# Two context blocks joined, gate rows by way of DRAM, a conditioning half split over two norms, and another order of MLP pieces

## The reference

```python
x = x + concat(diff_attention, dilated_attention) @ w_out      # first block
x = x + expert_choice_ffn(rms_norm(x))                         # 16 experts, 32 tokens each
x = rms_norm(x)

# second block, two layers i = 0, 1
mod   = silu(c)     @ ada_w[i] + ada_b[i]        # 6 rows of 1024: shift, scale, gate, twice
mod_c = silu(c_ctx) @ ada_w[i] + ada_b[i]
h, hc = x * (1 + sc1) + sh1, ctx * (1 + csc1) + csh1
y, yc = mixer_i(h, hc)                           # i=0: latent attention, i=1: neighbourhood attention
x     = layer_norm(alpha * x + g1 * y)
x     = layer_norm(alpha * x + g2 * mlp(x * (1 + sc2) + sh2))
# the context gets the same two steps in layer 0 only
mlp(h) = square(relu(h @ w1)) @ w2               # 1024 -> 4096 -> 1024
```

## Time and profile before

| | us |
|---|---|
| median of 3 runs (2580.91 to 2585.63) | 2583.34 |
| the profiled execution, its own time | 2582.17 |
| span of that execution in the trace | 2580.1 |

### The profile page before, as it was taken

One profiled execution on the slowest core, in us unless ns is written; L12 is line 12 of the kernel. 1 busy time (PEld: TensorE's weight loads), 2 busy tenths in 40 slices (PEclk: granted clock), 3 DMA queues, 4 the chain that ended last, 5 costly groups with the idle time before them and its releaser, 6 DMA issues.

```text
span 2580.1 us, 27920 instructions
## 1 busy us (share of the span) xinstructions
PE 2227.2 (86%) x11996; PEld 1171.1 (45%) x11996; DVE 534.1 (21%) x1018; ACT 236.8 (9%) x536; POOL 37.8 (1%) x109
## 2 busy tenths in 40 slices
PE   8987888888777888988888876599899999999998
PEld 6544343333333433433433322255466665445665
DVE  1332202221311011011011131224310030163002
ACT  1221101000100000000000000012110000061000
POOL 0000000000000000000000000000020000000000
PEclk9997899999999998999999988999999999999999
DMA  8766979999999999999999999964194431214540
GB/s 311 319 265 240 421 330 410 424 424 422 424 420 419 416 419 415 416 417 416 419 410 418 421 423 425 416 255 177 73 303 149 150 120 65 84 64 148 160 148 33
DMA packets 146564, 786.18 MB, mean 305 GB/s; under 512 B 11187, under 2 KB 66202, under 8 KB 93522
## 3 DMA queue, kind: packets, MB, share of 16 engines
q1 hardware_dynamic: 140104, 774.50, 74.7%
q10 hardware_dynamic: 6346, 9.95, 1.2%
HBM read 783.34 MB, written 6.12 MB: 306 GB/s over the span
## 4 chain that ended last, share of the span: by engine, by line
PE 71%; DMA 15%; DVE 7%; issue 2%; ACT 2%; SPq 2%; ACTq 0%; DVEq 0%
PE ps L285 14%; PE ps L1789 9%; PE ps L2197 9%; PE ps L2204 9%; DMA ring<-in_mlp_w 7%; DMA ring<-in_w_up 6%; PE ps L1757 5%; PE ps L318 4%; PE ps L1947 4%; PE ps L1762 3%; PE ps L1797 2%; PE ps L415 2%; DVE expert_work L1831 2%; PE ps L1809 2%; PE ps L1939 2%
## 5 line engine op out<-in xcount | busy, mean ns | idle before, releaser
L1757 PE MATMUL ps<-ring,xe 128*32 128x512 f32 x2048 | 297.9, 641 | 114.8 <-DMA ring<-in_w_up 41.1
L1789 PE MATMUL ps<-ring,expert_work 128*32 128x512 f32 x1408 | 247.4, 708 | 11.0 <-ACT expert_work L1818 11.0
L1762 PE MATMUL ps<-ring,xe 128*32 128x256 f32 x2048 | 204.9, 462 | 0.0
L1757 PEld LDWEIGHTS ps<-ring,xe 128*32 128x32 f32 x2048 | 61.1, 113 | 226.6 <-issue 97.6
L1762 PEld LDWEIGHTS ps<-ring,xe 128*32 128x32 f32 x2048 | 73.5, 111 | 168.3 <-issue 168.3
L1789 PEld LDWEIGHTS ps<-ring,expert_work 128*32 128x32 f32 x1408 | 60.6, 123 | 162.8 <-issue 140.0
L1947 PE MATMUL ps<-ring,c_qT 128*128 128x512 f32 x256 | 114.1, 598 | 10.3 <-DMA ring<-in_mlp_w 10.1
L1939 PE MATMUL ps<-hT,ring 128*128 128x256 f32 x512 | 114.8, 382 | 6.6 <-DMA ring<-in_mlp_w 6.6
L2197 PE MATMUL ps<-mlp_x_hT,ring 128*128 128x256 f32 x512 | 112.6, 379 | 1.9 <-DVE mlp_x_hT L366 1.9
L2197 PE MATMUL ps<-mlp_n_hT,ring 128*128 128x256 f32 x512 | 112.6, 379 | 1.8 <-DVE mlp_n_hT L366 1.8
L2204 PE MATMUL ps<-ring,mlp_x_h 128*128 128x512 f32 x256 | 111.8, 592 | 0.0
(11 more groups left out here) (399 smaller groups left out, 2118.2 us busy)
## 6 DMA issues: line engine op xcount, KB each, us to landing
ring<-in_w_gate SPq DMA_DIRECT2D x128, 1408.0 KB, 17.2
ring<-in_w_up SPq DMA_DIRECT2D x128, 1408.0 KB, 17.8
ring<-in_w_down SPq DMA_DIRECT2D x112, 1536.0 KB, 23.5
ring<-in_mlp_w SPq DMA_DIRECT2D x96, 1024.0 KB, 9.0
ring<-in_ada_w SPq DMA_DIRECT2D x32, 1536.0 KB, 12.1
ring<-in_w_in SPq DMA_DIRECT2D x8, 1536.0 KB, 19.0
ring<-in_na_w_qkv SPq DMA_DIRECT2D x12, 1024.0 KB, 8.3
ring<-in_w_down SPq DMA_DIRECT2D x16, 512.0 KB, 23.8
```

The source lines that it names most:

```text
L1757: nc.tensor.matmul(ps[32 * j:32 * j + 32, up, :], xe[:, k, :], w[:, :, 4 * j:4 * j + 4], start=(k == 0), stop=(k == KC - 1))
L1762: last = nc.tensor.matmul(ps[32 * j:32 * j + 32, 2, 256 * up:256 * up + 256], xe[:, k, :], two, start=(k == 0 and not up), stop=(k == KC - ...
L1789: last = nc.tensor.matmul(ps[32 * j:32 * j + 32, 1 - half, :], hgT[:, at:at + 32], w[:, (c - c0) * D + 512 * half:(c - c0) * D + 512 * hal ...
```

## The change

Four edits. (a) `uq` is planned behind (1, 3) and run whole after it; `ukv` behind and after (1, 10). (b) The four gates of x are written from `modc` to a DRAM tensor of 4 x 1024 numbers, two by ACT in stage 1, two by SP after NA's projections, and read back into `gB` with one broadcasting DMA each; `gate_jobs` for x is gone (the context's two stay). (c) Of the second conditioning half, pieces 8 to 11 stay behind the output projection; pieces 12 to 15 are planned behind all of mlp_x's pieces and run behind its last matmul, into banks 2 and 3; DVE adds them to the rows after the layer norm, PE waits for that before it transposes x, and the context's transposes use two banks in place of four. (d) `ORDER` takes the four w1 pieces of a turn and then the four w2 pieces, with a wait of PE for the relu and of ACT for the square two groups back.

```diff
+        SPLIT = 12
-        def ada_piece(pe, layer, i, base, bank0):
+        def ada_piece(pe, layer, i, base, bank0, first=0, last_k=KC - 1):
...
-                                        slot(n, N_IN)[:, ADA_W * b:ADA_W * b + ADA_W], start=(k == 0), stop=(k == KC - 1))
+                                        slot(n, N_IN)[:, ADA_W * b:ADA_W * b + ADA_W], start=(k == first), stop=(k == last_k))
...
-        CTX_AFTER = {(0, 8): ("dq",), (0, 12): ("dkv",), (1, 4): ("uq",), (1, 12): ("ukv",),
+        CTX_AFTER = {(0, 8): ("dq",), (0, 12): ("dkv",), (1, 3): ("uq",), (1, 10): ("ukv",),
...
         plan_mla(ids_x, "o")
-        plan_ada(1, 8, 16)
+        plan_ada(1, 8, SPLIT)
         TURN = 4
-        ORDER = [(1, 0), (1, 1), (2, 0), (1, 2), (2, 1), (1, 3), (2, 2), (2, 3)]
+        ORDER = [(1, 0), (1, 1), (1, 2), (1, 3), (2, 0), (2, 1), (2, 2), (2, 3)]
...
         mlp_x = plan_mlp(0)
+        plan_ada(1, SPLIT, 16)
...
+        gate_rows = nc.dram_tensor("gate_rows", [4, D], F32).ap()
+        GATES = ((0, 2), (0, 5), (1, 2), (1, 5))
+        def store_gate(eng, n):
+            layer, which = GATES[n]
+            dst = gate_rows[n:n + 1, :].rearrange("o (c p) -> p (o c)", p=P)
+            src = modc[:, layer, which * KC:which * KC + KC, 0:1].rearrange("p c o -> p (c o)")
+            eng.dma_start(dst, src, allow_slow_non_contiguous=True).then_inc(gate_stored, 16)
+        def load_gate(eng, n, gate):
+            eng.wait_ge(gate_stored, 32 if n < 2 else 64)
+            eng.dma_start(gate[:, :], gate_rows[n:n + 1, :].partition_broadcast(P).rearrange("q o d -> q (o d)"))\
+               .then_inc(gate_loaded.sem, 16)
...
             run_m.ev(act, "act")
+            act.wait_ge(v2.sem, v2.at("mod"))
+            store_gate(act, 0)
+            store_gate(act, 1)
             run_o.finished(act)
...
-                elif at == (1, 4):
-                    lat.pe_q(pe, 0, 4)
-                elif at == (1, 7):
-                    lat.run_uq.pe(pe, 4)
-                elif at == (1, 12):
-                    lat.pe_kv(pe, 0, MLA_HEADS)
-                elif at == (1, 15):
-                    lat.run_ukv.pe(pe, MLA_HEADS)
+                elif at == (1, 3):
+                    lat.pe_q(pe)
+                elif at == (1, 10):
+                    lat.pe_kv(pe)
...  (mixer_end)
-                run_gate.pe(pe)
-                run_gate.finished(pe)
...
-                run_gate.finished(dve)
+                dve.wait_ge(gate_loaded.sem, gate_at)
...  (mlp)
-                run_gate.pe(pe)
-                run_gate.finished(pe)
...
                     n = loop.arrived(pe, m, i)
+                    if g >= 2:
+                        pe.wait_ge(relu_done.sem, m * TURN + (rb + g - 1))
...
+                if beside:
+                    beside.pe_rest(pe)
...
-                run_gate.ev(act, "act")
+                load_gate(act, 2 * layer + 1, gB)
...
+                        if g >= 2:
+                            act.wait_ge(square_done.sem, m * TURN + (qb + g - 1))
...
+                    if beside and t == NT - 1:
+                        beside.dve_rest(dve)
...  (SecondHalf)
             def pe_sum(self, pe):
-                for i in range(KC, 2 * KC):
-                    ada_piece(pe, 1, i, ada1_base, 0)
+                for i in range(KC, SPLIT):
+                    ada_piece(pe, 1, i, ada1_base, 0, 0, SPLIT - KC - 1)
+            def pe_rest(self, pe):
+                for i in range(SPLIT, 2 * KC):
+                    ada_piece(pe, 1, i, ada1_base, 2, SPLIT - KC)
+            def dve_rest(self, dve):
+                dve.wait_ge(ada_done.sem, ada1_base + 2 * KC)
+                dve.wait_ge(self.rows_out, 1)
+                for b in range(2):
+                    row = self.rows[:, b, :]
+                    last = nc.vector.tensor_tensor(row, ps[:, 2 + b, 0:ADA_W], row, ALU.add)
+                last.then_inc(self.rows_out, 1)
...  (NA)
-        run_tc = Run(modulated(1, 0, 1, hT2, 0))
+        run_tc = Run(modulated(1, 0, 1, hT2, 0), (0, 1))
...
             run_tc.finished(pe)
+            pe.wait_ge(second_half.rows_out, 2)
             run_tx.pe(pe, normed)
...
+            run_n.finished(sp)
+            store_gate(sp, 2)
+            store_gate(sp, 3)
+            load_gate(sp, 2, gB)
             feed(sp)
```

More of the change, by code:

```diff
@@ L1293, in build @@
         mlp_n = plan_mlp(1)
+        gate_rows = nc.dram_tensor("gate_rows", [4, D], F32).ap()
+        gate_stored = sem("gate_rows_stored")
+        gate_loaded = Count(sem("gates_loaded"))
+        GATES = ((0, 2), (0, 5), (1, 2), (1, 5))
[8 more added lines that the diff above has]
+               .then_inc(gate_loaded.sem, 16)
+            gate_loaded.take(16)
         keep = ExitStack()
@@ L1310, in build @@
         a2 = Steps(sem("p2_act"), ["row2", "subsd"] + rms_names(NT) + ["ra"])
-        v2 = Steps(sem("p2_dve"), ["row3", "subvar", "sub", "var", "h", "lmax", "aff", "slot", "sel"])
+        v2 = Steps(sem("p2_dve"), ["row3", "subvar", "sub", "mod", "var", "h", "lmax", "aff", "slot", "sel"])
         run_ada = Run(ada_jobs(0, 0, rows0[:, 0:2, :]) + ada_jobs(0, 1, rows0[:, 2:4, :]))
@@ L2103, in mixer_end @@
             run_pre = Run(pre)
-            run_gate = Run(gate_jobs(layer, 2, s, gB), (4, 5))
             run_t = Run(transposes(KC, lambda t, c: o[:, t, c * P:(c + 1) * P], lambda c: oT[:, c, :]) if o is not None else [])
@@ L2107, in mixer_end @@
             a, v = Steps(sem(f"{name}_act"), ["pre", "ln_sd0", "ln_sd1"]), Steps(sem(f"{name}_dve"), ln_names())
+            gate_at = gate_loaded.n
             @block.tensor
@@ L2174, in mlp @@
             gB = sb(f"{name}_gate", [D], st)
-            run_gate = Run(gate_jobs(layer, 5, s, gB, "act"), (2, 3))
             run_t = Turned(x, lambda c: hT[:, c, :], lambda c: fold[:, 0, c:c + 1], lambda c: fold[:, 1, c:c + 1])
@@ L2282, in _ @@
                 for t in range(NT):
+                    if t == 0:
+                        dve.wait_ge(gate_loaded.sem, gate_loaded.n)
                     for half in range(2):
@@ L2337, in _ @@
             lat.act_up(act)
+            load_gate(act, 0, gB)
             lat.att.act(act)
```

6 lines of the change are left out of this document (2 added, 4 removed).

## The result

The changed kernel takes 2557.73 us (median of 4 runs, 2557.24 to 2565.53) and the kernel before 2584.49 (4 runs): ratio 0.9908, 95% interval 0.9894 to 0.9923. A second group of runs on another occasion gave 2558.82 (6 runs) and 0.9913 (0.9898 to 0.9928). The forecast was 2560. The profiled execution took 2557.49 us with a span of 2555.7, which is 24.4 us less than the span before; the forecast was 22.4 less.

What follows compares the result with a forecast made beforehand. DMA's load stream was taken to bound the experts, and a chain through PE with waits at four transitions the rest. Terms -5.7 - 3.3 - 2.9 - 1.0 - 11.6 + 2.1 = -22.4 us from 2582.2 gave 2560, range 2556 to 2564.

Steps and rivals of the forecast that it cites:

- The context blocks: Expert phase: earlier release of the ring's held slots shrinks two DMA holes; 5.7 us saved, bounds 0 and 12.6.
- the hole of (1 - 0.71) x 10 = 2.9 us: DMA hole at 380 to 390 us, at keys and values: it goes entirely, 2.9 us saved.
- The other hole: DMA hole at 340 to 350 us, at the context's queries: shrinks by 2.8 us.
- The gates at the end of latent attention and of NA: Gate matmuls leave PE at both ends: 3.3 us saved (bounds 2.0 and 4.7) and 2.9 us saved.
- The gate at mlp_n: Before mlp_n: first token half's eight transposes can run during the norm; 1.0 us saved, bounds 0 and 2.1.
- the second rival, the clock: Low clock lasts into the output projection and NA's projections, each losing some 2 to 3 us: 2565; chance 0.10.
- The conditioning: Output projection to mlp_x: four pieces there, not all, so the MLP starts earlier; 11.6 us saved, bounds 9 and 12.6.
- The 0.4 us for ACT's DMA issues: Before mlp_x: ACT's load issues hold its evacuations by up to 0.9 us, 0.4 taken.
- mlp_x's end: Between mlp_x and NA: the four moved conditioning pieces run there; 2.1 us lost, bounds 0.5 and 5.
- The MLP order: Inside the MLPs: no gap that another order could close; nothing, bounds -1 and +2.
- The stores: Gates' stores and loads through DRAM: both hide under other work; nothing taken, lower bound 0.
- the 62 us: Time from SP's last load of NA's stage to the first product needing the gate, as cover for the stores.

Runs made afterwards that it cites:

- ring: Kernel before with only the two context blocks moved and joined: 2575.8 us against 2582.74, ratio 0.9969.
- gates: Kernel before with only the four gates of x by way of DRAM: 2578.51 us, ratio 0.9977.
- tc4: Changed kernel with the context's transposes before NA through four banks, not two: 2560.97 us, ratio 0.992.
- warm6: Changed kernel with six matmuls of zeros in PE's gap before mlp_n: 2557.39 us, ratio 0.9904.
- split: Kernel before with only the conditioning half split over two norms, the new MLP order and the context's transposes in two banks: 2574.56 us, ratio 0.9964.
- again: Changed kernel once more, unedited: 2558.82 us.
- order: Kernel before with only the new order of the MLP's pieces and its waits: 2581.3 us, ratio 0.9997.
- old_order: Changed kernel with the MLP's new order and its waits undone: 2565.99 us, ratio 0.9942.
- fill: Changed kernel with matmuls of zeros: seven before stage 3, two at latent attention's end, three before mlp_n: 2555.45 us, ratio 0.9897.
- warmall: Changed kernel with matmuls of zeros: 14 before stage 3, five at latent attention's end, six before mlp_n: 2565.15 us, ratio 0.9928.

## Why the prediction was right, and where it was not

- **The context blocks** (5.7 us forecast, 7.65 in the trace, 8.0 by ring's ratio): mechanism and places right, size low. The step that failed is "the hole of (1 - 0.71) x 10 = 2.9 us". The busy share understates the hole: the rate in the same row is 272 of 424 GB/s, 0.64 and not 0.71, which makes it 3.6 us. The other hole, by bytes over 330 to 360 us (237 GB/s before, 282 after), shrank by 3.2 us and not 2.8 (3.0 in shares). 6.8 in all by the bytes moved by 400 us; the rest up to 8 lies within what executions differ by at the last expert (some 8 us among ten traces).
- **The gates at the end of latent attention and of NA** (3.3 and 2.9 forecast, 3.1 and 3.0 in the trace): right, with the reason given for the first: the transposes came at 0.50 and took 3.68 us for 16.
- **The gate at mlp_n** (1.0 forecast, 0.8 at the step): right in itself and wrong in effect. The step that failed is that the clock was put at nothing in the sum. I had the second rival, the clock, for the two projections behind the other gates and argued "mlp_n's start has like gaps" against it. They weren't alike once the gate's matmuls were gone. It cost 2.5 us in mlp_n. For the output projection the rival's mechanism came true in three other traces (gates, tc4 and warm6, 29.7 us and not 27.7), not in the changed kernel's.
- **The conditioning** (11.6 forecast, 12.2 in the trace; 10.5 in split): right, also in what is late next: ACT's two row copies. The 0.4 us for ACT's DMA issues wasn't needed: the issues run beside ACT's copies (the gate's load at 1852.59, the first window load at 1852.96, the copies at 1852.58 and 1852.97), and the second window load is issued by 1855.01, as the evacuations begin (1855.06).
- **mlp_x's end** (2.1 of loss forecast, 2.0 in the trace): right with some luck. The clock had fallen there in before (3.36 us for 16 transposes) and didn't in after. In split and again it fell too, and the loss is 3.3 us.
- **The MLP order** (nothing forecast, 0.9997 in order): right. That it must come with the split was in the working (the last turn's slots), and old_order shows 7 to 9 us for it. What failed here is small: "the new waits are for relus that had a whole piece of time". Three of the nine traces with the new order and the split near the norm have a wait of 0.78 to 1.34 us there; the last section has its rows.
- **The stores** (nothing): right. From the first store's issue to the load's it was 16.7 us, of which the issues themselves took 6.15; the packets by the earlier trace rows had said 10 us for the transfer. Two readings of rows were wrong without changing a term: `na_window`'s 2 x 1024 pieces have 876 bytes each and not 438, and a nearer row was the router's weights, 1024 pieces of 64 bytes that landed after 26.6 us. The Trainium skill, DMA: Bandwidth & Descriptors (its section Bandwidth and its rules for kernel authors), led to the prediction's estimate of 22 us for two stores with a descriptor for each element; the trace is below it, on the same side of the 62 us. The profiles agree with the Trainium skill's one descriptor per element: packets under 512 bytes went from 11187 to 15411, 4224 more, where the four gates have 4096 numbers; the other 128 I can't assign.
- **What was not in the sum** is the clock at stage 3 (-2.3; of five kernels before it or with one part changed, two show 141 to 142 us there and three 139.6) and at mlp_n (+2.5). The second is the edit's doing, the first is the chance of two executions. Without the first the traces would differ by 22.1 us, and that this is so near the forecast's 22.4 comes from another pair: mlp_n's loss of 2.5 and the 2.6 us by which the ring and the conditioning gave more than forecast. The total agrees better than its parts, and in that there is luck.

## What to carry to other kernels

Work on PE that looks removable can be what keeps its clock up: before taking it out of a gap of a few us, read the granted clock behind the gap, and fill the gap (no longer than it is) if it falls. Then read it again further on: at mlp_n the filler brought 2.4 us in the traces, before stage 3 it only moved the fall. Price a hole in a transfer stream by the bytes in it, not by the busy share. And when loads are prefetched across a loop's end, the order in which the last turn frees its slots is part of the change, even where it is worth nothing inside the loop.

## What the runs showed of the hardware

- **The same code, two clocks.** Stretches of PE work with no edit in them came out at two lengths from one execution to another: 139.56 or 141 to 142 us for stage 3 to latent attention's end, 220.5 or 222.2 for mlp_x, 199.7 or 201.9 for NA. Where the longer one came, windows showed 0.50 near its start, behind gaps of 1 to 8 us on PE, and 1.00 again later; the three traces of the next point are the exception. So a difference of 2 us between two single traces means nothing until the clock has been read on both sides.
- **ACT's DMA issues can hold a relu.** In fill, warmall and again mlp_x is 1.1 to 1.6 us longer with the clock at 1.00. With the MLP's new order PE runs its third w1 piece at once and waits for the first relu; ACT is still issuing the norm's loads. In these three the issues end 13.7 to 14.3 us after mlp_x's first matmul and PE waits 0.78 to 1.34 us at its third piece; in the six other traces with the new order and the split they end at 12.1 to 12.9 us, and PE doesn't wait. Why such an issue takes 5.4 us or more here, and 0.34 in before, isn't shown. ACT and PE in fill:

```profile
1856.45 6.85 ACTq L1511 DMA_DIRECT2D lnb<-in_ln_g  x1
1863.34 2.57 ACTq L1511 DMA_DIRECT2D lnb<-in_ln_b  x1
1866.43 1.09 ACT L2283 ACTIVATE mlp_x_relu<-ps 128x512 f32<-128x512 f32 x2 [12.93 <-PE ps L2215]
...
1867.08 14.08 PE L2215 MATMUL ps<-mlp_x_hT,ring 128*128 128x256 f32 x64 [1.18 <-ACT mlp_x_relu L2283]
```

- **Issue of 4-byte stores.** The same store of 1024 single elements, 4 KB, held ACT's queue for 0.39 and 0.60 us and SP's, behind weight loads, for 2.83 and 3.28 us.
- **DVE and POOL side by side.** With POOL's tables moved behind the conditioning they meet DVE's gain of x. POOL's 16 operations took 18.24 us and not 14.71, and DVE's 1024-wide products of two SBUF tiles 1.84 to 2.04 us:

```profile
2085.46 18.24 POOL L2444 TENSOR_TENSOR ring<-na_window,cst 128x384 f32<-128x384 f32 x16
...
2091.66 2.04 DVE L850 TENSOR_TENSOR x<-x,lnb 128x1024 f32<-128x1024 f32 x1
2093.74 1.84 DVE L851 TENSOR_TENSOR x<-x,lnb 128x1024 f32<-128x1024 f32 x1
```

In the kernel before, the same operations took 1.23 us, as they do in the changed kernel at mlp_x's start, where POOL is idle:

```profile
2114.75 1.23 DVE L850 TENSOR_TENSOR x<-x,lnb 128x1024 f32<-128x1024 f32 x1
```

The Trainium skill, SBUF — State Buffer (Who interferes with whom), says that a DVE instruction with two inputs in SBUF and a GpSimd instruction that reads SBUF exclude one another, the second waiting for the first to end. The trace agrees: DVE's 1.23 us grow by up to 0.81, less than one POOL operation of 0.92. NA's projections hid all of it (196.72 us, the old length less the gate).
